# A fourth size class for the experts of a MoE layer on one NeuronCore: 65 to 96 tokens as 64 + 32

## The reference, cut to what matters

```python
logits = h @ w_router + b_router                 # 32 experts
top_val, top_idx = lax.top_k(logits, 4); gates = softmax(top_val)
for each expert e, on the tokens that chose it:
    gu  = h[tok] @ w_gu[e] + b_gu[e]             # 1024 -> 2048
    glu, lin = split(gu);  glu = min(glu, 7);  lin = clip(lin, -7, 7)
    act = glu * sigmoid(1.702 * glu) * (lin + 1)
    y[tok] += gate * (act @ w_down[e] + b_down[e])   # 1024 -> 1024
```

```
61 23 30 21 58 27 62 31 10 69 17 11 45 39 72 11 32 96 21 49 61 55 42 50 22 42 50 12 14 77 21 49
```

## Time and profile before

| | |
|---|---|
| median of three runs | 1286.19 us (1285.8 to 1289.31) |
| the profiled execution | 1288.51 us, of which the span from first to last instruction is 1286.3 us |
| mean granted TensorE clock | 0.949 |
| TensorE busy | 1132.5 us, 88% of the span |
| VectorE busy | 417.8 us, 32% |
| ScalarE busy | 195.4 us, 15% |
| moved by the DMA queues | 454.88 MB, mean 354 GB/s |
| experts | from 306.5 us to the end |

### The profile page before, as it was taken

One profiled execution on the slowest core, in us unless ns is written; L12 is line 12 of the kernel. 1 busy time (PEld: TensorE's weight loads), 2 busy tenths in 40 slices (PEclk: granted clock), 3 DMA queues, 4 the chain that ended last, 5 costly groups with the idle time before them and its releaser, 6 DMA issues.

```text
span 1286.3 us, 20674 instructions
## 1 busy us (share of the span) xinstructions
PE 1132.5 (88%) x6676; PEld 496.9 (39%) x6677; DVE 417.8 (32%) x1283; ACT 195.4 (15%) x419; POOL 43.9 (3%) x27
## 2 busy tenths in 40 slices
PE   4999998967877788799999998999999989869997
PEld 0667664643332222244333443443333333214432
DVE  2133735342333323312522224223332233331233
ACT  2323242141100000001111011010111011001110
POOL 0141101010000000000000000000000000000000
PEclk9998999986998999899999989999999999989898
DMA  9963229622999999999999989989999999999992
GB/s 379 347 228 141 68 85 373 258 86 109 420 421 422 422 422 422 421 422 400 410 422 422 422 323 417 423 339 421 422 423 421 422 421 423 421 423 421 405 394 106
DMA packets 76882, 454.88 MB, mean 354 GB/s; under 512 B 9868, under 2 KB 14732, under 8 KB 24524
## 3 DMA queue, kind: packets, MB, share of 16 engines
q1 hardware_dynamic: 70304, 449.76, 85.8%
q10 hardware_dynamic: 6540, 4.60, 1.3%
HBM read 451.17 MB, written 3.17 MB: 353 GB/s over the span
## 4 chain that ended last, share of the span: by engine, by line
PE 67%; DMA 20%; DVE 4%; issue 4%; ACT 2%; SPq 2%; POOL 0%; DVEq 0%; ACTq 0%
PE psum L867 24%; DMA ring<-w_gu 16%; PE psum L904 14%; PE psum L567 6%; PE psum L923 4%; PE psum L836 3%; PE psum L776 3%; PE psum L576 2%; DMA ring<-w_down 2%; SPq L481 2%; DMA ring<-w_ada 2%; PE psum L531 1%; PE psum L844 1%; PE psum L860 1%; PE psum L878 1%
## 5 line engine op out<-in xcount | busy, mean ns | idle before, releaser
L867 PE MATMUL psum<-ring,work 128*32 128x512 f32 (+2 forms) x2048 | 432.5, 621 | 34.0 <-DMA ring<-w_gu 32.5
L867 PEld LDWEIGHTS psum<-ring,work 128*32 128x32 f32 (+2 forms) x2048 | 131.6, 133 | 286.1 <-issue 196.6
L904 PE MATMUL psum<-ring,work 128*32 128x256 f32 (+2 forms) x1504 | 219.5, 480 | 18.8 <-issue 10.4
L1619 DVE SCALAR_TENSOR_TENSOR x<-psum,tiny,x 128x256 f32<-128x256 f32 (+1 forms) x512 | 155.2, 377 | 213.7 <-PE psum L923 213.7
L1588 DVE TENSOR_SCALAR work<-csb 96x128 bf16<-96x128 f32 x64 | 15.4, 280 | 403.0 <-PE psum L867 402.0
L980 ACT ACTIVATE work<-psum 128x256 f32<-128x256 f32 (+6 forms) x207 | 88.5, 443 | 345.7 <-PE psum L904 220.7
L904 PEld LDWEIGHTS psum<-ring,work 128*32 128x32 f32 (+2 forms) x1504 | 87.7, 130 | 136.4 <-issue 109.6
L1236 ACT ACTIVATE work<-work 128x128 f32<-128x128 f32 (+2 forms) x64 | 25.0, 391 | 573.2 <-DVE work L1602 573.2
L567 PE MATMUL psum<-h,ring 128*128 128x320 f32 x320 | 91.3, 443 | 1.2 <-ACT h L1015 1.2
L923 PE MATMUL psum<-work 32*128 32x320 f32 (+2 forms) x512 | 83.1, 481 | 1.4 <-ACT work L980 1.1
L567 PEld LDWEIGHTS psum<-h,ring 128*128 128x128 f32 x320 | 62.0, 195 | 26.9 <-issue 1.6
(11 more groups left out here) (209 smaller groups left out, 615.8 us busy)
## 6 DMA issues: line engine op xcount, KB each, us to landing
ring<-w_gu SPq DMA_DIRECT2D x256, 1024.0 KB, 20.6
ring<-w_down SPq DMA_DIRECT2D x128, 1024.0 KB, 18.9
ring<-w_ada SPq DMA_DIRECT2D x12, 2048.0 KB, 9.3
ring<-w_in SPq DMA_DIRECT2D x7, 2048.0 KB, 29.9
ring<-w_out SPq DMA_DIRECT2D x2, 2048.0 KB, 11.5
x<-xT SPq DMA_DIRECT2D x1, 1280.0 KB, 6.0
yT<-x SPq DMA_DIRECT2D x2, 640.0 KB, 3.9
work<-b_exp ACTq DMA_DIRECT2D x3, 384.0 KB, 16.4
```

What stands on the lines that cost most here:

```text
L867: last = mm(o, xg[:, kk, 0:m], cols(ring[:, kk, :]), start=False, stop=kk == KD - 1)
L904: last = mm(o, actT[:, kk, 0:m], ring[:, GU_UNITS + kk // 2, c1_:c1_ + n], start=False, stop=kk == 7)
L1619: last = stt(x[:, f, cols], bank[SPREAD_BANKS[u]][:, cols], mod[:, 40 + f, sq_:sq_ + 1], x[:, f, cols], ALU.mult, ALU.add)
```

## The change

A fourth class, `groups` 3, for experts of 65 to 96 tokens. `by_size` has one more comparison on the side of the large ones; `by_rows` is the old three-way choice, still used for gathering and turning the tokens, where these experts keep the form with 128 columns.

In the new class tokens 0 to 63 (`PART_A`) go through two column groups of 64 and tokens 64 to 95 (`PART_B`) through four of 32. Each stage of gate and up takes its rows (3, 3, 2) first for part B and then again for part A; units are released in the second walk. Down does so with four of its eight rows at a time. The two parts have PSUM banks of their own; gate and up of part B stand side by side in one bank. The scatter sums the two parts: for each block of features a product with 64 rows and one with 32 rows into the same bank. The picks with gates exist twice (`wpick_b`, `spread_b`). The activations are handled as 512 and 256 columns of work where the largest class has 512 and 512.

The core of the diff:

```diff
         def by_size(eng, n, b, body):
+            with eng.If(n > b * CAP + CAP // 2):
+                with eng.If(n > b * CAP + CAP * 3 // 4):
+                    body(1)
+                with eng.Else():
+                    body(3)
+            with eng.Else():
+                with eng.If(n > b * CAP + CAP // 4):
+                    body(2)
+                with eng.Else():
+                    body(4)
...
+            PART_A, PART_B = slice(0, 64), slice(64, 96)
             def up_bias(turn, groups):
                 pe.wait_ge(eh_up_ready, turn + 1)
-                for o, cols in up_blocks(groups):
-                    mm(o, eh[0:3 * NE, 0, 0:CAP // groups], cols(b3[0:3 * NE, 0:2 * D]), start=True, stop=False)
+                for m, blocks in ((32, up_blocks(4, U + 2)), (64, up_blocks(2))) if groups == 3 else ((CAP // groups, up_blocks(groups)),):
+                    for o, cols in blocks:
+                        mm(o, eh[0:3 * NE, 0, 0:m], cols(b3[0:3 * NE, 0:2 * D]), start=True, stop=False)
             def gate_up(k0, k1, turn, groups):
+                if groups == 3:
+                    for kk in range(k0, k1):
+                        pe.wait_ge(unit_full[kk], turn * 16 + 16)
+                        for o, cols in up_blocks(4, U + 2):
+                            mm(o, xg[:, kk, PART_B], cols(ring[:, kk, :]), start=False, stop=kk == KD - 1)
+                    for kk in range(k0, k1):
+                        for o, cols in up_blocks(2):
+                            last = mm(o, xg[:, kk, PART_A], cols(ring[:, kk, :]), start=False, stop=kk == KD - 1)
+                        last.then_inc(gu_used, 1)
+                    return
...
             def down(turn, groups):
                 pe.wait_ge(at_ready, turn * 2 + 2)
+                if groups == 3:
+                    for k0 in (0, 4):
+                        for kk in range(k0, k0 + 4):
+                            if kk % 2 == 0:
+                                pe.wait_ge(unit_full[GU_UNITS + kk // 2], turn * 16 + 16)
+                            down_rows(kk, PART_B, *down_blocks(4, DN + 1))
+                        for kk in range(k0, k0 + 4):
+                            last = down_rows(kk, PART_A, *down_blocks(2))
+                            if kk % 2:
+                                last.then_inc(dn_used, 1)
+                    return
...
-            def turn_pick(turn):
-                for tt, (t0, n) in enumerate(TILES):
-                    last = nc.tensor.transpose(bank[DN + 1][0:CAP, t0:t0 + n], wpick[0:n, tt, :], ident[0:n, 0:n])
+            def turn_pick(turn, groups):
+                pe.wait_ge(wpick_ready, turn * 3 + 3)
+                for bk, from_ in ((DN + 1, wpick), (U + 3, wpick_b)) if groups == 3 else ((DN + 1, wpick),):
+                    for tt, (t0, n) in enumerate(TILES):
+                        last = nc.tensor.transpose(bank[bk][0:CAP, t0:t0 + n], from_[0:n, tt, :], ident[0:n, 0:n])
...
             def scatter(i, turn, groups):
+                def part(u, f, groups, c, by, start, stop):
+                    m = CAP // groups
+                    g = f * groups // 8
+                    c0_ = c + f * P - g * (D // groups)
+                    rows_ = slice(m * g, m * (g + 1))
+                    return mm(bank[SPREAD_BANKS[u]][:, 0:T], otok[rows_, c0_:c0_ + P], by[rows_, :], start=start, stop=stop)
                 for u in range(4):
                     if i:
                         pe.wait_ge(acc_ready, turn * 8 + (u + 1))
+                    if groups == 3:
+                        part(u, FEATURES[4 * i + u], 2, 0, spread, True, False)
+                    else:
+                        part(u, FEATURES[4 * i + u], groups, 0, spread, True, True).then_inc(sc_ps, 1)
+                if groups == 3:
+                    for u in range(4):
+                        part(u, FEATURES[4 * i + u], 4, 512, spread_b, False, True).then_inc(sc_ps, 1)
...
@@ ScalarE @@
                     if i == 0:
                         act_.wait_ge(str_ps, turn + 1)
-                        copy(spread, bank[7][:, 0:T]).then_inc(spread_ready, 1)
+                        last = copy(spread, bank[7][:, 0:T])
+                        if groups == 3:
+                            last = copy(spread_b, bank[5][:, 0:T])
+                        last.then_inc(spread_ready, 1)
```

More of the change, by code:

```diff
@@ L198, in build @@
         spread = take4(T)
+        spread_b = take4(T)
         lgT = spread
@@ L383, in build, with halves @@
         SEQ = ((slice(0, TP), 0), (slice(TP, T), 1))
+        def halves(groups):
+            if groups == 3:
+                return slice(0, 512), slice(512, 768)
+            n = CHC // groups
+            return slice(0, n), slice(n, 2 * n)
         def expert_units(e):
@@ L887, in down_bias @@
             def down_bias(turn, groups):
-                n, blocks = down_blocks(groups)
                 pe.wait_ge(eh_down_ready, turn + 1)
-                if groups == 1:
+                if groups in (1, 3):
                     pe.wait_ge(spread_ready, turn + 1)
+                for part, bk in ((4, DN + 1), (2, DN)) if groups == 3 else ((groups, DN),):
+                    n, blocks = down_blocks(part, bk)
+                    for o, c0_ in blocks:
+                        mm(o, eh[0:3 * NE, 1, 0:CAP // part], b3[0:3 * NE, 2 * D + c0_:2 * D + c0_ + n], start=True, stop=False)
@@ L892, in down_bias, with down_rows @@
+            def down_rows(kk, cols, n, blocks):
                 for o, c0_ in blocks:
-                    mm(o, eh[0:3 * NE, 1, 0:CAP // groups], b3[0:3 * NE, 2 * D + c0_:2 * D + c0_ + n], start=True, stop=False)
+                    c1_ = kk % 2 * D + c0_
+                    last = mm(o, actT[:, kk, cols], ring[:, GU_UNITS + kk // 2, c1_:c1_ + n], start=False, stop=kk == 7)
+                return last
             def down(turn, groups):
-                m = CAP // groups
-                n, blocks = down_blocks(groups)
@@ L901, in down @@
                         pe.wait_ge(unit_full[GU_UNITS + kk // 2], turn * 16 + 16)
[L902 to L904 removed]
+                    last = down_rows(kk, slice(0, CAP // groups), *down_blocks(groups))
                     if kk % 2:
                         last.then_inc(dn_used, 1)
[L908 to L910 removed]
+            def turn_pick(turn, groups):
[3 more added lines that the diff above has]
+                        last = nc.tensor.transpose(bank[bk][0:CAP, t0:t0 + n], from_[0:n, tt, :], ident[0:n, 0:n])
@@ L1260, in outputs @@
                     last = copy(otok.rearrange("p (b n) -> p b n", b=2), psum[:, 6:8, :])
+                elif groups == 3:
+                    copy(otok[:, 0:512], bank[6])
+                    last = copy(otok[:, 512:768], bank[7][:, 0:256])
                 else:
@@ L1592, in glu @@
                 v.wait_ge(gu_used, turn * 8 + 8)
-                n = CHC // groups
-                for i in range(2):
-                    h_ = slice(i * n, (i + 1) * n)
-                    if groups == 1:
+                for i, h_ in enumerate(halves(groups)):
+                    n = h_.stop - h_.start
+                    if groups == 3:
+                        g_, l_ = (bank[2], bank[3]) if i == 0 else (bank[4][:, 0:256], bank[4][:, 256:512])
+                    elif groups == 1:
                         g_, l_ = bank[2 + i][:, :], bank[4 + i][:, :]
@@ L1628, in start @@
                 one_hots(0, e, eh_up_ready)
-                by_size(v, n, b, lambda groups: picks(turn, e, groups))
+                by_rows(v, n, b, lambda groups: picks(turn, e, groups))
             def expert(turn, e, b, begins, ends):
@@ L1637, in expert @@
                     one_hots(0, e + 1, eh_up_ready)
-                    by_size(v, after, b, lambda groups: picks(turn + 1, e + 1, groups))
+                    by_rows(v, after, b, lambda groups: picks(turn + 1, e + 1, groups))
                 if not begins:
```

80 lines of the change are left out of this document (42 added, 38 removed).

## The result

The changed kernel takes 1277.18 us (median of 8 runs, 1272.25 to 1283.6) beside 1287.67 for the kernel before; the ratio is 0.9921, 95% interval 0.9900 to 0.9942. The forecast was 1259.0 us, with a range of 1252 to 1270, a gain of 27.2 us. The gain came out at 10.5 us: the right sign, outside the range. In two later lots its median was 1273.53 and 1278.27.

What follows compares the result with a forecast made beforehand. Transfers bound it almost everywhere, TensorE in large experts and at the end. 17.1 us of queue idle plus 10.6 in expert 29 less 0.5 scatter gave 27.2 off the 1286.2 median: 1259.0 us, 8-in-10 range 1252 to 1270.

Steps and rivals of the forecast that it cites:

- What bounds the kernel: Whole kernel: transfers at 422 GB/s bound it almost everywhere; TensorE behind the four large experts, with 20.5 us of idle queue.
- Gate and up, 6.4 us: Expert 29's gate and up: three rows take 8.15 us instead of 10.57, times 8/3 stages, 6.4 us saved.
- Down, 4.0: Expert 29's down: from 16.27 us to between 11.15 and 13.0, a saving of 3.3 to 5.1, taken as 4.0.
- The bound of 13.0: Expert 29's down: its upper time, if as much is lost to the half clock as before.
- Together 10.6: Expert 29 on TensorE: 6.4 gate and up, 4.0 down, 0.8 activations, less 0.6 turning picks; bounds 9.5 to 12 us.
- Scatter, 0.5 lost: A large expert's scatter, inside the next expert's time: between 0.5 us gained and 1.5 lost, taken as 0.5 lost.
- The idle of the queues goes wholly, 17.1 us: DMA queues behind experts 9, 14 and 17: all idle time vanishes, so expert 29 starts 17.1 us earlier, at 1153.2.
- The drains of changing column groups: Rival, 9%: ten column-group changes per expert cost up to 0.61 us each, 6 us, leaving 4.6 saved per expert; 1270 us.
- The loop's code is too long: Rival, 8%, slower: TensorE's loop body of 1690 instructions is not kept, each turn fetches again; 1294 or 1345 us.
- Nothing is added on SyncE; on ScalarE and VectorE a copy and three picks: Work added on other engines: none on SyncE; a copy and three picks per large expert, beside work of TensorE.

## Why the prediction was wrong, step by step

- *What bounds the kernel* (transfers almost everywhere, TensorE behind the four large experts): right. The dips went, and the queues move 421 to 423 GB/s in slices 12 to 38.
- *Gate and up, 6.4 us*: each walk is right to the hundredth, but for the first, which had the clock at half. *Down, 4.0*: 5.3 (16.27 to 10.97) in expert 29. The prediction took the middle between a clock that falls and one that stays. In this trace it stayed in experts 14, 17 and 29 and fell in expert 9, below, with granted clocks of 1.00 and 0.86. The wait for VectorE ahead of it had shrunk from 1.45 + 0.58 us to 0.47, but it is 0.47 in front of the slow one too, so which way it goes is open. Over the eight traces that use the new class at full weight traffic, 8 of 32 downs take 12.3 to 12.6 us and 24 take 10.9. (The bound of 13.0 in the prediction leaves out the 0.4 for two more pieces.) *Together 10.6*: 11.6 (53.7 to 42.1).

```profile
603.48 12.60 PE L941 MATMUL psum<-ring,work 128*32 128x256 f32 x96 [0.22 <-issue]
...
754.66 10.97 PE L941 MATMUL psum<-ring,work 128*32 128x256 f32 x96 [0.17 <-issue]
```

- *Scatter, 0.5 lost*: the halves take 2.10 instead of 2.42, and 0.72 is lost to VectorE behind them. Right in size.
- *The idle of the queues goes wholly, 17.1 us*: right at all three, and the 3.4 us behind expert 29 went too.
- *The drains of changing column groups* (9%): wrong; 10.97 against 10.75 leaves 0.2 us for two further walks, no more than a block's own edge. The Trainium skill, "TensorEngine Tiling (Array Packing)", Key Properties, names a drain for each change of tiling mode and no price; this trace neither shows the drain by itself nor leaves room for more than 0.1 us a change.
- *The loop's code is too long* (8%): the nearest rival, and wrong in its form. The body is kept at 1690: 31 packets, not hundreds, and none from 382 to 1230 us, and the middle experts still take 27.8 and 28.8 us. What I priced was fetching in every turn or never.
- **The step that failed** is the sum's silence on the first walk. "Nothing is added on SyncE; on ScalarE and VectorE a copy and three picks" is where the added parts are listed, and TensorE's longer code (7373 instructions up to the pass's end against 5578, 32% more) has no term there. In its place the runs showed 14 to 15 us lost by the code's presence (the run in which the class is never taken). In that run's trace expert 0 takes 5 us more than before, expert 1 about 8, and expert 31 has a stall of 3.56. What the sum does price held: the use of the class gains 29.6 us where 27.2 were forecast. The row for the missing term was on the table: 3.90 us for the one long stall in the first walk of the loop. A likely reason for it is that expert 1 jumps over two classes' pieces to its own, and the new pieces (24 matmuls in a stage of gate and up, 48 in down) lie in that jump; no run here moves a piece without changing the length of the code, so this stays open. Read as a price for each, with the four or five stalls that the traces show now, it would have given 15 to 20 us and a forecast in the 1270s; their number was not in any row of before.
- The Trainium skill, "Runtime: NRT & Kernel Launch", Instruction fetch mechanics, says that a taken branch to code outside a window of two pages stalls, and also that crossing a block of 256 instructions is mostly hidden. The traces agree with the first for code entered the first time and not for code of earlier turns; they disagree with the second in expert 31, where a stall of 3.54 us stands within a piece, with no branch at that place.

## What to carry to other kernels

A class that is chosen at run time can have a price even where it is never taken; here it was 14 to 15 us. Where a loop's body is walked for the first time while DMA queues are full, count its instructions, skipped pieces included, and put a price on such stalls from a row of the trace. Ask first what can go before adding a piece: here the gain stayed and 11 to 16 us of loss went away, the larger part (7.3 us) with the largest class, which the new class replaces for these counts, and the rest with shared code and passes of 96 or with the spread between lots. And where a ring of weights paces the kernel, a saving on TensorE is worth the idle of the queues that it removes and whatever it moves at the end; that part of the forecast held within 1 us for expert 29 and within 2.4 us for the whole.

## What the runs showed of the hardware

- Code walked for the first time cost TensorE stalls, the four longest of the changed kernel 2.9 to 5.2 us, each with one packet of instructions in it. Three of them stood beside queues at 412 to 421 GB/s, and with an eighth of the weight traffic they fell to at most 0.8 us. The fourth, ahead of the first down in the loop, stood beside 98 GB/s; with the lighter traffic, 5 GB/s there, it was still 3.2. Why that one stays is open.
- A stall can cost more than its length: behind the 3.54 us in expert 31 the granted clock was 0.68 over 7.9 us, and the work there took 3.1 us longer.
- A loop body of 1690 instructions of TensorE was kept over its later turns: no packet of instructions came from 382 to 1230 us. One packet is 256 instructions (7 more packets for 1795 more).
- Walks in two and in four column groups may alternate at about 0.1 us a change or less (10.97 us against 7.09 + 3.66, two further walks).
- The first 306 us, the same code in each kernel, end anywhere between 306.4 and 312.3 us. Single executions of one kernel differ by about as much.
